# Output gates of a recurrence: projected with the weights standing, applied where the turned output leaves PSUM

## What is computed

```python
def project(h):
    q, i_in, f_fw, f_bw, z = jnp.split(h @ w_in, 5, axis=-1)
    ...
    return heads(jax.nn.silu(q)), heads(i_in), gates, z

def readout(o, z):
    o = _rmsnorm(o, o_gain).reshape(B, L, D_INNER).astype(z.dtype)
    return (o * jax.nn.silu(z)) @ w_out
```

## Time and profile before

| | |
|---|---|
| time, median of 3 runs | 1853.02 us (1852.6 to 1854.72) |
| span of the profiled execution | 1852.8 us |
| PE, PE's weight loads | 97%, 88% of the span |
| DVE, ACT, POOL | 67%, 49%, 3% of the span |
| mean granted TensorE clock | 0.997 of full speed |
| the recurrence groups | from about 930 to 1560 us |

### The profile page before, as it was taken

One profiled execution on the slowest core, in us unless ns is written; L12 is line 12 of the kernel. 1 busy time (PEld: TensorE's weight loads), 2 busy tenths in 40 slices (PEclk: granted clock), 3 DMA queues, 4 the chain that ended last, 5 costly groups with the idle time before them and its releaser, 6 DMA issues.

```text
span 1852.8 us, 30204 instructions
## 1 busy us (share of the span) xinstructions
PE 1796.3 (97%) x12082; PEld 1625.3 (88%) x12082; DVE 1237.6 (67%) x1621; ACT 907.0 (49%) x1104; POOL 49.8 (3%) x51
## 2 busy tenths in 40 slices
PE   6999999999999999999999999999999999999998
PEld 5877799988987799988989899898989987899896
DVE  4878655546778665546476867667686786477874
ACT  5565533335575443335444545344453453366772
POOL 2000000001000000000000000000000000000130
PEclk9999999999999999999999999999999999999999
DMA  8558477554557656653322122212222222153113
GB/s 194 177 190 283 142 186 195 195 187 142 168 187 255 189 160 187 194 188 105 91 80 67 60 69 69 59 58 80 58 68 69 69 69 97 64 190 100 46 48 113
DMA packets 273243, 238.40 MB, mean 129 GB/s; under 512 B 32288, under 2 KB 242240, under 8 KB 272848
## 3 DMA queue, kind: packets, MB, share of 16 engines
q1 hardware_dynamic: 271872, 233.21, 41.5%
q0 software_dynamic: 1232, 3.25, 0.7%
HBM read 235.39 MB, written 1.05 MB: 128 GB/s over the span
## 4 chain that ended last, share of the span: by engine, by line
PE 85%; DVE 6%; ACT 3%; DVEq 2%; DMA 1%; issue 1%; ACTq 1%; SPq 1%
PE pg L2530 35%; PE pg L1252 33%; PE pm L1252 11%; PE pm L2530 4%; PE pm L1255 2%; DMA ring<-in_w_in 1%; DVE ring_r L566 1%; PE pm L2533 1%; DVEq L1731 1%; ACT ring_r L559 1%; DVE work L1742 1%; SPq L2142 0%; DVE ring_r L1695 0%; DVE ring L1729 0%; DMA ring<-in_mla_w_in 0%
## 5 line engine op out<-in xcount | busy, mean ns | idle before, releaser
L566 DVE TENSOR_TENSOR ring_r<-ring,ring_r 128x2048 fp32r<-128x2048 f32 (+1 forms) x126 | 283.6, 2260 | 159.5 <-ACT ring_r L559 153.9
L2530 PE MATMUL pg<-ring_r,work_r 128*128 128x512 f32 (+1 forms) x1776 | 381.2, 373 | 5.4 <-DVEq L3005 2.9
L1252 PE MATMUL pg<-ring_r,work_r 128*128 128x256 f32 (+3 forms) x1792 | 380.8, 323 | 2.1 <-DVE work_r L1701 1.0
L2530 PEld LDWEIGHTS pg<-ring_r,work_r 128*128 128x128 f32 x1776 | 306.9, 189 | 66.9 <-issue 7.8
L1252 PE MATMUL pg<-ring_r 128*128 128x256 f32 (+3 forms) x1008 | 328.5, 326 | 4.8 <-DVEq L784 2.0
L2530 PE MATMUL pg<-work_r,ring_r 128*128 128x256 f32 x2688 | 318.7, 281 | 7.0 <-DVE ring_r L566 3.9
L2530 PEld LDWEIGHTS pg<-work_r,ring_r 128*128 128x128 f32 x2688 | 317.3, 188 | 8.5 <-DVE ring_r L566 4.8
L1252 PEld LDWEIGHTS pg<-ring_r,work_r 128*128 128x128 f32 x1792 | 301.0, 190 | 26.4 <-issue 2.8
L559 ACT ACTIVATE ring_r<-ring 128x2048 fp32r<-128x2048 f32 (+1 forms) x126 | 237.2, 1890 | 177.0 <-DMA ring<-in_w_ffn_up 72.1
L1252 PE MATMUL pg<-work_r,ring_r 128*128 128x512 f32 (+1 forms) x976 | 264.0, 360 | 0.0
L1252 PEld LDWEIGHTS pg<-ring_r 128*128 128x128 f32 x1008 | 191.9, 190 | 19.3 <-DVEq L784 3.0
(11 more groups left out here) (387 smaller groups left out, 2083.4 us busy)
## 6 DMA issues: line engine op xcount, KB each, us to landing
ring<-in_hg_w_in SPq DMA_DIRECT2D x80, 512.0 KB, 3.9
ring<-in_w_in SPq DMA_DIRECT2D x36, 1024.0 KB, 5.1
ring<-in_ada_w SPq DMA_DIRECT2D x24, 1024.0 KB, 7.5
ring<-in_w_ffn_gate SPq DMA_DIRECT2D x44, 512.0 KB, 4.0
ring<-in_w_ffn_up SPq DMA_DIRECT2D x44, 512.0 KB, 5.4
ring<-in_w_ffn_down SPq DMA_DIRECT2D x22, 1024.0 KB, 4.9
ring<-in_w_out SPq DMA_DIRECT2D x12, 1024.0 KB, 6.3
ring<-in_ple_w_gate SPq DMA_DIRECT2D x8, 1024.0 KB, 4.9
```

The lines of the kernel that those rows point to most:

```text
L566: W.low_done(V.tensor_tensor(lo, W.raw(i, name)[:, 0:lo.shape[1]], W.hi(i, name).bitcast(f32), ALU.subtract))
L1252: return T.matmul(out_, lhsT, rhs, start=first, stop=last)
L2530: return T.matmul(out_, lhsT, rhs, start=first, stop=last)
```

## The change

`z` is now projected as `gf`, `gb` and `q` are, with the weights standing and the 512 tokens moving, so it comes out with head columns on the partitions, turned as `oT` is. ACT's `silu` writes it to the place in `oT` (`head_rows`) where the turned output will be put. The gating of `o` before the normalisation is gone. ACT squares the output out of PSUM without waiting for DVE. DVE's last multiplication of the normalisation reads PSUM itself and releases `o`. The new `out_gated`, on DVE, takes the turned output out of PSUM, multiplies it by the gain and by the gate, and writes the product over the gate; it releases `oT`. It stands behind all of level 1's work of the following group, and for the last group behind the groups. ACT's `out_transposed` is gone. The loads of z's weights change their pattern with the projection.

```diff
+        def head_rows(g):
+            groups = oT.rearrange("p (g n) -> p g n", g=NG)
+            return groups[:, g, :] if isinstance(g, int) else groups[:, bass.ds(g, 1), :].rearrange("p a n -> p (a n)")
...
-                        rows, cols_ = (slice(4 * half, 4 * half + 4), slice(0, 256)) if name[0] in "vz" else (slice(0, KC), slice(P * half, P * half + P))
+                        rows, cols_ = (slice(4 * half, 4 * half + 4), slice(0, 256)) if name[0] == "v" else (slice(0, KC), slice(P * half, P * half + P))
...
-                    q=(q_in(b), ACT.Silu, 1.0, h_q), v=(v_in(b), ACT.Copy, 1.0, h_v), z=(z_in, ACT.Silu, 1.0, h_z),
+                    q=(q_in(b), ACT.Silu, 1.0, h_q), v=(v_in(b), ACT.Copy, 1.0, h_v), z=(head_rows(n * 2 + b), ACT.Silu, 1.0, h_z),
...
-            def out_transposed(g):
-                HM.wait_filled(act, "oT", g)
...
-                HM.release(A.activation(dst, HM.buf("oT"), ACT.Copy, scale=p_ogain), "oT")
-                h_oT.set(act.drain())
...
             def heads_high(a, b):
+                h_oT.wait(act, (b - 1) // GH)
...
-                if prev is not None:
-                    out_transposed(prev)
                 keys_of_level(n, b, 2)
...
+                HM.wait_filled(act, "o", g)
                 for j in range(J):
-                    if j % 4 == 0:
-                        h_oz.wait(act, g, j // 4 + 1)
...
-                if name in ("v", "z"):
+                if name == "v":
...
-                elif name not in ("v", "z"):
+                elif name != "v":
                     HS.used(last, pieces[half])
...
+            def out_gated(g):
+                HM.wait_filled(dve, "oT", g)
+                h_z.wait(dve, g)
+                HM.release(V.scalar_tensor_tensor(head_rows(g), HM.buf("oT"), p_ogain, head_rows(g), ALU.mult, ALU.mult), "oT")
+                h_oT.set(dve.drain())
...
+                    if prev is not None and lev == 1:
+                        out_gated(prev)
                     if nxt and lev == 6:
                         keys(*nxt)
...
-                HM.wait_filled(dve, "o", g)
-                h_z.wait(dve, g)
-                for k in range(2):
-                    cs = slice(k * 512, (k + 1) * 512)
-                    h_oz.set(V.tensor_tensor(o_[:, cs], HM.buf("o")[:, cs], z_in[:, cs], ALU.mult))
...
-                HM.release(V.tensor_scalar(st_b[:, 0:J], st_a[:, 0:J], 1.0 / P, EPS, ALU.mult, ALU.add), "o")
+                V.tensor_scalar(st_b[:, 0:J], st_a[:, 0:J], 1.0 / P, EPS, ALU.mult, ALU.add)
...
-                V.tensor_tensor(j3(o_), j3(o_), bc(st_c, [J, P], 2), ALU.mult)
+                HM.release(V.tensor_tensor(j3(o_), j3(HM.buf("o")), bc(st_c, [J, P], 2), ALU.mult), "o")
...
+            dve.wait_ge(loaded_on, 32)
             all_groups(dve, group)
+            out_gated(NG - 1)
```

More of the change, by code:

```diff
@@ L623, in program @@
         array = lambda ap, k: ap[:, k * 1024:(k + 1) * 1024]
-        k_both, z_in = raw3[:, 4, :], raw3[:, 5, :]
+        k_both = raw3[:, 4, :]
         maps = w2.take(1024)
@@ L694, in program @@
         HGEMM = Turns(pg, sem("hg_gemm_filled"), [sem("hg_gemm_free0"), sem("hg_gemm_free1")], PAIR, ahead=True)
-        hg_last_of = {n: n[:-3] + n[-1] for n in pair_pieces if n[0] in "vz" or n[-3] == "1"}
+        hg_last_of = {n: n[:-3] + n[-1] for n in pair_pieces if n[0] == "v" or n[-3] == "1"}
         HS = Split(thousands(ring_r[:, 0:4096]), thousands(ring_r[:, 4096:8192]), sem("hg_high_ready"), dict(dve=sem("hg_low_ready")),
@@ L730, in program @@
         h_S, h_map, h_og, h_oT = Event("hg_states"), Event("hg_maps"), Event("hg_out_normed"), Event("hg_oT_in")
-        h_oz, h_sq = Event("hg_out_gated", 2), Event("hg_out_squares")
+        h_sq = Event("hg_out_squares")
         h_free = Event("hg_raw_used")
@@ L850, in second_sp @@
                         sp.sem_inc(steps_apart, 1)
-                        rows, cols_ = (slice(4 * half, 4 * half + 4), slice(0, 256)) if name[0] in "vz" else (slice(0, KC), slice(P * half, P * half + P))
-                        dst = HW.slot(f"{name}_{b}").rearrange("p (c n) -> p c n", n=256 if name[0] in "vz" else P)
+                        rows, cols_ = (slice(4 * half, 4 * half + 4), slice(0, 256)) if name[0] == "v" else (slice(0, KC), slice(P * half, P * half + P))
+                        dst = HW.slot(f"{name}_{b}").rearrange("p (c n) -> p c n", n=256 if name[0] == "v" else P)
                         HW.loaded(sp.dma_start(dst, hg_w[which, n * 2 + b, :, rows, cols_]), f"{name}_{b}")
@@ L950, in keys_of_level @@
                 h_klev.set(act.drain())
-            def out_transposed(g):
-                HM.wait_filled(act, "oT", g)
-                dst = oT.rearrange("p (g n) -> p g n", g=NG)
-                dst = dst[:, g, :] if isinstance(g, int) else dst[:, bass.ds(g, 1), :].rearrange("p a n -> p (a n)")
-                HM.release(A.activation(dst, HM.buf("oT"), ACT.Copy, scale=p_ogain), "oT")
-                h_oT.set(act.drain())
             def piece_high(name):
@@ L1047, in second_act @@
             evac(0, 0, "z")
-            act.wait_ge(loaded_on, 16)
             all_groups(act, group)
-            out_transposed(NG - 1)
             heads_high(14, 16)
@@ L1877, in second_dve @@
             heads_low(14, 16)
-            dve.wait_ge(loaded_on, 32)
             dve.wait_ge(m_gtb, 1)
```

## The result

| | before | changed |
|---|---|---|
| median of the runs, us | 1852.81 (4 runs, 1851.28 to 1854.72) | 1890.73 (4 runs, 1886.68 to 1893.11) |
| ratio, 95% interval | | 1.0201 [1.0189, 1.0213] |
| span of the profiled execution, us | 1852.8 | 1884.5 (its own time 1886.68) |

The changed kernel is 2% slower. The forecast of 1873.8 us had the sign right and the size wrong: the time lies 17 us above it and 10 us above the range. The profiled execution is the fastest of the four. The mean granted clock of its core is 0.991; the other three have 0.988 to 0.990. That turns out to be a large part of the story. Further down, one execution of each of the two kernels with a late release took far longer (2020 and 3609 us); the ratios leave these two out.

What follows compares the result with a forecast made beforehand. PE was taken to bound the recurrence. Level 2's wait 19.6, level 0's 3.6 and the end 0.3, less 2.1 and 0.6 for cheaper z, gave 20.8 us on 1853.0: 1873.8 us, range 1867 to 1881.

Steps and rivals of the forecast that it cites:

- Level 2's wait: PE's level 2 in groups 1 to 7 waits for DVE's gate instruction to release the turned output: 19.6 us.
- Level 0's wait: Next group's level 0 waits for DVE's normalising multiplication to release the output's half of pm: 4.6 us, net 3.6.
- unit 9: Half of z projected on PE ahead of the next group's level 0; 0.30 us cheaper, gained where no wait is left.
- z, 0.30 per half: PE's projection of each half of z takes 5.54 us instead of 5.84, saving 0.30 us.
- The end, 0.3: End of the recurrence: last turned output passes DVE then ACT instead of ACT alone, 0.3 us more.
- The loop's second pass: PE's 1.01 us stand ahead of level 1 there was to shrink by 0.7 us, since PE comes later.
- The clock, rival 4: PE's clock falls in the new standing time: one fall gives 1877.2 us, one in each of seven 1897.6; 8%.

Runs made afterwards that it cites:

- the two kernels with a late release: Kernel before, only ACT's copy releasing the turned output moved later: behind gf's evacuation, 1890.22 us; behind q0's split, ahead of that evacuation, 1864.04 us.
- the split moved: Changed kernel, gate still in level 1, DVE's split for the group after next moved ahead of the diagonal's masked copy: 1877.78 us, ratio 1.0130.
- the gate at level 0: Changed kernel with DVE's gate instruction one level earlier, behind its level 0 work instead of level 1: 1857.63 us, ratio 1.0022.

## Why the prediction was wrong

- **Level 2's wait, 19.6 us: right.** The table has 21.5 us, of which PE stood 0.95 in group 7 before as well; 20.5 are new. The instruction costs 1.28 as taken. The pause ahead of it, taken as 0.15, is 0.20 us in groups 5 and 6, but 0.40 in groups 1 and 3 and 0.76 to 0.78 in groups 2 and 4. In these four, the loop's, DVE's sequencer has register instructions in front of it; why two of them pause longer is open. So groups 2 and 4 stand 3.2 us. Taking groups 1 and 6 for all six missed that.
- **Level 0's wait: right in kind, 1 us too much.** 5.4 us of waits less the seven 0.3 of unit 9 is 3.3. The forecast had 4.6 - 0.3 = 4.3 before it took 0.7 off for the loop's second pass.
- **z, 0.30 per half: right within 0.03 us** (5.54 and 5.57 against 5.84). The 0.06 us that the Trainium skill ("TensorE: Matmul & The Clock Gate", section "Back-to-back issue gap") would have given is out; the section itself calls its formula that of an isolated matmul.
- **The end, 0.3: right** by the one wait that was read (1.2 us against 0.9).
- **The loop's second pass: wrong sign.** I wrote that PE "that comes 0.7 us later stands 0.7 less there". It stands on "issue" for 2.6 us instead of 1.1. The 1.01 us ahead of level 1 did go, so of the pass only 0.5 us is lost besides level 0's wait. It brought a fall of its own, though.
- **The clock, rival 4, given 8%: this is the step that failed.** The forecast took PE's clock as full through new stands of 2.7 to 3.7 us. The runs show seven falls, which cost 10.8 us in the profiled execution. The rows that spoke for a full clock were stands of about 1 us. The one row that had a stand of that length, 3.08 us, had a fall, and it was given too little weight. It is not a like case, though: 24 matmuls of two columns stood ahead of it, and the clock fell at 439.93 us, 0.25 us into the stand. The size per fall was off as well, in the other direction. I took 7 us at a clock of 0.52 as 3.4 us lost, but PE was busy for only 3.67 of those 7 us, which makes 1.8; the falls here cost 1.4 to 1.7. With the clock's term the sum would have been 1873.8 + 10.8 = 1884.6, 2 us under the profiled run and 6 us under the median.

The Trainium skill ("TensorE: Matmul & The Clock Gate", Part 1) was cited for a fall that may come in some runs and not in others. The runs bear this out: group 3's stand had no fall at 2.81 us in the changed kernel and one at 2.80 with the split moved, and the loop's had one at 2.62 us in the changed kernel and none at 2.46 with the gate at level 0. But the same page of the Trainium skill, "TensorE: Matmul & The Clock Gate", has a section "HAM oscillation — how this bites in real kernels", which describes a kernel that pays the half clock anew in every repetition of its loop because PE waits once in each. This case is of that kind, and I had not weighed it. The trace agrees: seven falls, six of them at the seven stands of level 2.

## What to carry to other kernels

A wait that is put between dense stretches of PE can be priced twice: its length, and half of the time that PE then works at half clock. Here the second price came with most stands of 2.2 us and more, and with none of 1.0 to 1.5 us. Before summing waits, look in the trace for the stand of PE nearest in length to the new one and at the granted clock behind it. When a release moves to another engine, look for the place in that engine's order, not only for its duration: the same 1.28 us instruction cost 33 us more behind level 1 than one level earlier, in idle time.

## What the runs showed that was not expected

- **Length of the stand and the clock.** In the recurrence of the ten profiles of this case, none of the 15 stands of PE of 1.0 to 1.5 us had a fall, in the stand or just behind it, and 24 of the 28 of 2.2 us and more had one. Of two of 1.82 us, one had. It is a count from one kernel, not a law. Filling the stand with work that is thrown away won 6 us net.
- **The loop's branch.** Where level 0 waited 0.8 us just ahead of the loop's second pass, PE's first matmul of that pass came 2.2 to 2.6 us late on "issue" (four profiles). Without that wait it was 0.7 to 1.4 us (six profiles). A wait there seems to be paid again behind the branch. Which part of the issue makes it so was not tried.
